# Attention: unnormalized probabilities into the product with v, made token by token, divided as it leaves its bank, and transposed

## The reference, cut to what matters

```python
s_lat = jnp.where(mask[None, :, None, None], s_lat, -jnp.inf)
s_ctx = jnp.einsum('bnqkgd,bskd->bnkgqs', qb, k_ctx).astype(jnp.float32) * ATTN_SCALE
logits = jnp.concatenate([s_lat, s_ctx, sink_logits(sink, s_lat.shape)], axis=-1)
p = jax.nn.softmax(logits, axis=-1).astype(v.dtype)
o = (jnp.einsum('bnkgqs,bnskd->bnqkgd', p[..., :n_band], vb)
     + jnp.einsum('bnkgqs,bskd->bnqkgd', p[..., n_band:-1], v_ctx))
return o.reshape(B, L, ATTN_DIM) @ w_o
```

## Time and profile before

| what | value |
|---|---|
| median of 3 runs | 3303.78 us (3301.16 to 3306.16) |
| profiled execution, its own time | 3303.78 us |
| span of the profiled execution | 3301.9 us |
| PE busy | 3066.8 us, 93% |
| PE weight loads | 2819.7 us, 85% |
| DVE busy | 2154.3 us, 65% |
| ACT busy | 1140.0 us, 35% |

### The profile page before, as it was taken

One profiled execution on the slowest core, in us unless ns is written; L12 is line 12 of the kernel. 1 busy time (PEld: TensorE's weight loads), 2 busy tenths in 40 slices (PEclk: granted clock), 3 DMA queues, 4 the chain that ended last, 5 costly groups with the idle time before them and its releaser, 6 DMA issues. The chain is left out here.

```text
span 3301.9 us, 48081 instructions
## 1 busy us (share of the span) xinstructions
PE 3066.8 (93%) x19222; PEld 2819.7 (85%) x19222; DVE 2154.3 (65%) x2879; ACT 1140.0 (35%) x1941; POOL 574.5 (17%) x578
## 2 busy tenths in 40 slices
PE   5999869999999999999999998679999999969999
PEld 4999658999899898998999897468998999858998
DVE  4776486777776656776876535657777777485444
ACT  3222454223422424223322433234224222454222
POOL 1112101112111111112111102642112112201001
PEclk8999899999999999999999998679999999999999
DMA  7666414666565445665665443024665666313443
GB/s 262 201 206 183 142 46 133 195 218 188 182 196 171 110 127 186 197 208 169 199 209 148 122 126 103 15 68 155 218 195 153 218 208 199 107 43 90 128 128 96
DMA packets 565507, 515.75 MB, mean 156 GB/s; under 512 B 42965, under 2 KB 499238, under 8 KB 563494
## 3 DMA queue, kind: packets, MB, share of 16 engines
q1 hardware_dynamic: 565286, 512.68, 50.8%
HBM read 509.37 MB, written 3.24 MB: 155 GB/s over the span
## 5 line engine op out<-in xcount | busy, mean ns | idle before, releaser
L1342 PE MATMUL bank<-h_hi,w_hi 128*128 128x384 f32 x3328 | 1114.9, 335 | 0.0
L1344 PE MATMUL bank<-h_hi,w_lo 128*128 128x384 f32 x3328 | 1113.7, 335 | 0.0
L1343 PE MATMUL bank<-h_lo,w_hi 128*128 128x384 f32 x3328 | 1113.2, 334 | 0.0
L1745 DVE TENSOR_TENSOR w_lo<-raw,w_hi 128x1024 fp32r<-128x1024 f32 x648 | 805.4, 1269 | 418.2 <-ACT w_hi L1591 413.0
L1591 ACT ACTIVATE w_hi<-raw 128x1024 fp32r<-128x1024 f32 x648 | 679.4, 1060 | 995.7 <-PE bank L1375 483.4
L1767 DVE SCALAR_TENSOR_TENSOR fold<-ada_raw,cond,fold 128x1024 f32<-128x1024 f32 x462 | 638.6, 1439 | 0.0
L1342 PEld LDWEIGHTS bank<-h_hi,w_hi 128*128 128x128 f32 x3328 | 625.1, 188 | 6.9 <-issue 1.2
L1343 PEld LDWEIGHTS bank<-h_lo,w_hi 128*128 128x128 f32 x3328 | 625.0, 188 | 5.8
L1344 PEld LDWEIGHTS bank<-h_hi,w_lo 128*128 128x128 f32 x3328 | 624.9, 188 | 0.0
L2057 POOL TENSOR_TENSOR h_lo<-tmp,h_hi 128x384 fp32r<-128x384 f32 x176 | 283.9, 1613 | 1799.6 <-DVE h_hi L1793 1799.6
L1371 PE MATMUL bank<-w_hi,h_hi 128*128 128x512 f32 x1056 | 334.2, 397 | 0.0
(11 more groups left out here) (198 smaller groups left out, 2422.4 us busy)
## 6 DMA issues: line engine op xcount, KB each, us to landing
raw<-w_ffn_in SPq DMA_DIRECT2D x352, 512.0 KB, 5.0
ada_raw<-w_ada SPq DMA_DIRECT2D x272, 512.0 KB, 4.2
raw<-w_ffn_out SPq DMA_DIRECT2D x176, 512.0 KB, 4.5
raw<-w_hgrn_in SPq DMA_DIRECT2D x40, 512.0 KB, 4.9
g_rows<-g_dram SPq DMA_DIRECT2D x12, 1024.0 KB, 6.8
raw<-w_attn_qkv SPq DMA_DIRECT2D x24, 512.0 KB, 5.9
raw<-w_conv_in SPq DMA_DIRECT2D x24, 512.0 KB, 4.7
ada_first<-w_ada SPq DMA_DIRECT2D x16, 512.0 KB, 10.8
```

The costliest lines, as they stand in the source:

```text
L1342: mm(out, wh, h_hi[:, k, :], start=(k == 0), stop=False)
L1343: mm(out, wh, h_lo[:, k, :], start=False, stop=False)
L1344: last = mm(out, wl, h_hi[:, k, :], start=False, stop=(k == DC - 1))
L1745: V.tensor_tensor(w_lo[:, b % RING, :], raw[:, b % RAW, :], w_hi[:, b % RING, :].bitcast(F32), ALU.subtract).then_inc(w_lo_made, 1)
```

## The change

The exponentials go to PE undivided. `turn_probs` waits for `prob_made` and no more for `p_normed`. `values(c)` has its operands exchanged: the transposed probabilities, 128x128, are the weights, 64 columns of v move, and the result has tokens on partitions and both heads' 2 x 64 features beside each other, for three token blocks, always in bank 6. The 14 products remain 14; `tile_position` is gone. DVE's `normalize` is replaced by `inverse(c)`, the sums and the reciprocal of both heads into `over`, and `scale_out(c)`, one multiplication of 384 elements from bank 6 into `tmp` with the reciprocals broadcast. PE's new `turn_out(c)` transposes the three 128x128 blocks of `tmp` into bank 7, from which ACT and DVE make `o_hi` and `o_lo`. The loops have one step more (`DC + 3`).

```diff
@@ pe_core
-            pe.wait_ge(p_normed, n + 1)
+            pe.wait_ge(prob_made, n + 1)
...
-            if c >= 2:
-
-                pe.wait_ge(o_lo_made, DC * mi + c - 1 + CREDIT)
-            bank = psum[6 + c % 2]
+            if c >= 1:
+
+                pe.wait_ge(o_scaled, DC * a + c)
             cols = slice(g * HD, (g + 1) * HD)
-            key = [vt[:, 1, cols], vt[:, 2, cols], vc[:, cols]]
+            latent = [vt[:, 1, cols], vt[:, 2, cols], vc[:, cols]]
             for x in range(2):
...
+                for b, (kt, keys) in enumerate(((0, latent), (3, [vt[:, 0, cols]]), (4, latent))):
+                    lo = P * b + HD * x
+                    for k, key in enumerate(keys):
+                        last = mm(psum[6][:, lo:lo + HD], pt[(2 * c + x) % 3][:, (kt + k) * P:(kt + k + 1) * P], key,
+                                  start=(k == 0), stop=(k == len(keys) - 1))
             last.then_inc(pv_done, 1)
 
-        for j in range(DC + 2):
+        def turn_out(c):
+            pe.wait_ge(o_scaled, DC * a + c + 1)
+            if c >= 1:
+
+                pe.wait_ge(o_lo_made, DC * mi + c + CREDIT)
+            for b in range(3):
+                last = nc.tensor.transpose(psum[7][:, TILE_OF[b] * P:(TILE_OF[b] + 1) * P],
+                                           tmp[:, c % 2, b * P:(b + 1) * P], ident)
+            last.then_inc(o_turned, 1)
+
+        for j in range(DC + 3):
             if j < DC:
                 scores(j)
+            if j >= 3:
+                turn_out(j - 3)
             if 1 <= j <= DC:
                 turn_probs(2 * j - 2)
-            if j >= 2:
+            if 2 <= j < DC + 2:
                 values(j - 2)
@@ act_core
-        for j in range(DC + 2):
+        for j in range(DC + 3):
+            if j >= 3:
+                c = j - 3
+                act.wait_ge(o_turned, DC * a + c + 1)
+                A(o_hi[:, c, :], psum[7][:, 0:T], ACT.Copy).then_inc(mix_hi_made, 1)
...
-            if j >= 2:
-                c = j - 2
-                act.wait_ge(pv_done, DC * a + c + 1)
-                A(o_hi[:, c, :], psum[6 + c % 2][:, 0:T], ACT.Copy).then_inc(mix_hi_made, 1)
@@ dve_core
-        def normalize(h):
...
+        def inverse(c):
+            dve.wait_ge(prob_made, HEADS * a + 2 * c + 2)
...
+            r = over[:, c % 2, :, 0:3]
+            V.tensor_tensor(r, soft[:, :, 6:9], soft[:, :, 9:12], ALU.add).then_inc(soft_step, 1)
+            dve.wait_ge(soft_step, 2 * (DC * a + c) + 1)
+            V.reciprocal(r, r).then_inc(soft_step, 1)
+
+        def scale_out(c):
+            dve.wait_ge(pv_done, DC * a + c + 1)
+            dve.wait_ge(soft_step, 2 * (DC * a + c) + 2)
+            if c >= 2:
+                dve.wait_ge(o_turned, DC * a + c - 1)
+            r = over[:, c % 2, :, 0:3].rearrange("p x b -> p b x").unsqueeze(3).to_broadcast([P, 3, 2, HD])
+            V.tensor_tensor(tmp[:, c % 2, :].rearrange("p (b x d) -> p b x d", b=3, x=2),
+                            psum[6][:, 0:T].rearrange("p (b x d) -> p b x d", b=3, x=2), r,
+                            ALU.mult).then_inc(o_scaled, 1)
...
             if j < DC:
                 maxima(2 * j + 1)
-                normalize(2 * j)
+            if 2 <= j < DC + 2:
+                scale_out(j - 2)
             if 1 <= j <= DC:
                 copy_probs(2 * j - 1)
+            if j >= 3:
+                c = j - 3
...
+                V.tensor_tensor(o_lo[:, c, :], psum[7][:, 0:T], o_hi[:, c, :].bitcast(F32),
+                                ALU.subtract).then_inc(o_lo_made, 1)
             if j < DC:
-                normalize(2 * j + 1)
...
+                inverse(j)
```

More of the change, by code:

```diff
@@ L355, in build @@
     SEG_AT = (0, T, T + P)
+    TILE_OF = (1, 0, 2)
     KEYS = sum(SEG)
@@ L378, in build @@
     soft = put("soft", [P, 2, 16])
+    over = put("over", [P, 2, 2, 4])
     rot_m = attn_k[:, 0:P]
@@ L390, in build @@
     sink8_made, score_done, score_read, neg_made = sem("sink8_made"), sem("score_done"), sem("score_read"), sem("neg_made")
-    prob_made, soft_step, p_normed, pt_done = sem("prob_made"), sem("soft_step"), sem("p_normed"), sem("pt_done")
-    pt_copied_v, pt_copied_a, pv_done = sem("pt_copied_v"), sem("pt_copied_a"), sem("pv_done")
+    prob_made, soft_step, o_scaled, pt_done = sem("prob_made"), sem("soft_step"), sem("o_scaled"), sem("pt_done")
+    pt_copied_v, pt_copied_a, pv_done, o_turned = sem("pt_copied_v"), sem("pt_copied_a"), sem("pv_done"), sem("o_turned")
     STEPS = HEADS + 3
@@ L536, in values @@
             pe.wait_ge(pt_copied_a, HEADS * a + 2 * c + 2)
-            if c >= 2:
-                pe.wait_ge(o_lo_made, DC * mi + c - 1 + CREDIT)
-            bank = psum[6 + c % 2]
+            if c >= 1:
+                pe.wait_ge(o_scaled, DC * a + c)
             cols = slice(g * HD, (g + 1) * HD)
-            key = [vt[:, 1, cols], vt[:, 2, cols], vc[:, cols]]
+            latent = [vt[:, 1, cols], vt[:, 2, cols], vc[:, cols]]
             for x in range(2):
[L544 to L554, removed]
-            last.then_inc(pv_done, 1)
-        for j in range(DC + 2):
+                for b, (kt, keys) in enumerate(((0, latent), (3, [vt[:, 0, cols]]), (4, latent))):
[3 more added lines that the diff above has]
+                                  start=(k == 0), stop=(k == len(keys) - 1))
+            last.then_inc(pv_done, 1)
+        def turn_out(c):
[7 more added lines that the diff above has]
+        for j in range(DC + 3):
             if j < DC:
                 scores(j)
+            if j >= 3:
+                turn_out(j - 3)
             if 1 <= j <= DC:
                 turn_probs(2 * j - 2)
-            if j >= 2:
+            if 2 <= j < DC + 2:
                 values(j - 2)
@@ L766, in copy_probs @@
             V.tensor_copy(pt[h % 3][:, 0:512], psum[4][:, :]).then_inc(pt_copied_v, 1)
-        def normalize(h):
[L769 to L780, removed]
+        def inverse(c):
+            dve.wait_ge(prob_made, HEADS * a + 2 * c + 2)
+            if c >= 2:
+                dve.wait_ge(o_scaled, DC * a + c - 1)
+            r = over[:, c % 2, :, 0:3]
[5 more added lines that the diff above has]
+            dve.wait_ge(soft_step, 2 * (DC * a + c) + 2)
+            if c >= 2:
+                dve.wait_ge(o_turned, DC * a + c - 1)
[3 more added lines that the diff above has]
+                            ALU.mult).then_inc(o_scaled, 1)
+        for j in range(DC + 3):
             if j < DC:
@@ L786, in dve_core @@
                 maxima(2 * j + 1)
-                normalize(2 * j)
+            if 2 <= j < DC + 2:
+                scale_out(j - 2)
             if 1 <= j <= DC:
                 copy_probs(2 * j - 1)
-            if j < DC:
-                normalize(2 * j + 1)
[L792 to L796, removed]
+            if j >= 3:
+                c = j - 3
+                dve.wait_ge(mix_hi_made, DC * mi + c + 1)
+                V.tensor_tensor(o_lo[:, c, :], psum[7][:, 0:T], o_hi[:, c, :].bitcast(F32),
+                                ALU.subtract).then_inc(o_lo_made, 1)
+            if j < DC:
+                inverse(j)
         dve.wait_ge(out_stored, 16 * stores_until(s + 1))
```

## The result

The changed kernel took 3322.15 us (median of 4 runs, 3321.32 to 3325.38) against 3303.05 us before (4 runs, 3301.16 to 3306.16): a ratio of 1.0058, 95% interval 1.0043 to 1.0073. It is slower by 0.6%, 19 us. The forecast was 3308 with a range to 3316, so it missed, on the side of its first rival and beyond that rival's price. Steps and queues came out nearly as laid out; TensorE's clock at the cores' end did not.

The account below looks back on a forecast made before the run. The prediction took DVE to bound the attention cores before and PE's loop over ACT after. Start, steps and end summed to +2.6 us in the first core and +1.5 in the second: 3303.8 + 4.1 = 3308, range 3302 to 3316.

Parts of the forecast that it names:

- What bounds the kernel now: Attention cores: DVE, busy 7.17 of 7.47 us, sets the step; all working is on 133.7 us of both cores.
- DVE, part by part: DVE's work in a step falls to 5.67 us; if DVE alone decided, 1.8 us a step saved.
- PE, part by part: PE's step becomes 6.92 us, values taking 3.12 instead of 1.53, so PE becomes the bound.
- rival 2: Gaps between PE blocks belong to semaphore waits: 0.15 kept per new block, loop 7.5, time 3313; chance 0.13.
- Rival 3: In values, 128-column loads hide and 64 moving columns decide: 1.5 us, step 6.1, time 3289; chance 0.04.
- The loop that closes: Round of turn_probs, values, turn_probs, exponentials and copy makes a step 7.22 us; five steps 36.1 instead of 37.3.
- the 0.03 among its signs: Expected in the profile after: in each step, PE's turn_probs waits for ACT's pt by 0.03.
- The start: Steps 0 to 2 of each core: 0.94 us shorter, 14.0 in the first core, 14.4 in the second.
- rival 4: Low-clock stretch in the start moves: 0.8 us a core gained or 3.6 lost; inside the range, no own chance.
- The end: Last step's first maxima to projection: 18.56 us instead of 13.84 and 15.0, clock taken as staying at 1.00.
- Rival 1: Clock falls in the new end too: values(6) 3.1 us more per core, 4 with longer drop, 3315; chance 0.14.
- The sum: Cores 68.7 and 69.1 us against 66.1 and 67.6: +4.1 us on 3303.8, so 3308.

Follow-up runs that it names:

- e3_no_divide: Kernel before with the multiplications of pr by the reciprocals left out, turn_probs waiting for the exponentials alone, old values: 3293.4 us, ratio 0.9967.
- e2_wide_v: Changed kernel with each product of values streaming v's 64 columns twice, 128 moving columns: 3312.3 us, ratio 1.0025 against the kernel before.
- e5_both_orders: Changed kernel with ACT's copy of head 2j-1 before head 2j+1's exponentials and DVE's o_lo before its copy: 3297.8 us, ratio 0.9981 against the kernel before.
- e4_act_order: Changed kernel with only ACT's copy of head 2j-1 moved ahead of the exponentials of head 2j+1: 3302.2 us, one run, no ratio.
- e9_late_turns: e5_both_orders with turn_out(6) behind values(7) and turn_out(7) behind the projection's first block on PE: 3295.9 us, ratio 0.9976 against the kernel before.
- e1_fill_end: Changed kernel with unread identity transposes (11, 5, 11, 10) in PE's four pauses at the core's end: 3310.0 us, ratio 1.0017 against the kernel before.
- e11_wide_end: Changed kernel with v streamed twice, 128 moving columns, in values(6) and values(7) alone: 3312.4 us, ratio 1.0021 against the kernel before.
- e8_before_fill: Kernel before with 22 identity transposes in PE's one long pause at the core's end, before turn_probs(14): 3302.8 us, ratio 0.9994.

## Why the prediction was wrong, point by point

- **What bounds the kernel now**: right. DVE is busy 7.17 of the 7.47 us, and e3_no_divide shows that relieving it helps: 6.94.
- **DVE, part by part**: right. scale_out 0.56 against 0.55; DVE busy 5.71 of a step against 5.67.
- **PE, part by part**: right. 28 records in 3.08 us, 0.110 each, against 3.12 (28 x 0.112 is 3.14), and e2_wide_v shows that the load decides. The gap belongs to the shape change and not to the wait: none stands before `values`; rival 2 falls. Rival 3 wanted 1.5 us for the 28 records and falls too. Scores with its gap measured 1.73 against 1.80. PE's own step is 6.82 (e5_both_orders) against 6.92.
- **The loop that closes**: right, 7.22 forecast and 7.29 measured. PE's wait for ACT is 0.29 us, which is the forecast's 7.22 - 6.92 = 0.30; the 0.03 among its signs does not fit its own sum. Five steps took 37.0 in the first core, where one step was 7.5 and one 7.6, and 36.5 in the second, against 36.1. e4_act_order removes the loop by one line.
- **The start**: 14.0 and 14.4 forecast, 13.7 and 13.0 measured. One low stretch of the second core's start did not come, rival 4's case. Its price was 0.8; between the two cores of the changed kernel, one with it and one without, it is 0.7 in the start and 1.2 up to the last step's maxima, and 1.6 in e9_late_turns.
- **The end**: here it failed, in the sentence "so I take the clock as staying at 1.00". The work and waits were right: with the clock up the end is 18.67 us (e1_fill_end) against 18.56, and the first two pauses were 1.34 and 0.64 against 1.5 and 0.8. The clock fell in both cores.
- **Rival 1** named the mechanism with a chance of 0.14 and a price of 3 to 4 us a core. The price was 7 us a core (13.9 over both), and another 1.2 in the projection's first group. It was sized for values(6) alone, as the low stretches of before, 3.4 and 6.8 us, would cover it; their `values` moved 128 columns. The new low stretch, 20.5 us, also covers turn_probs(15), turn_out(6), values(7) and turn_out(7). This is the mis-sized term, and e11_wide_end shows what it hangs on: with 128 moving columns it is 3.4 us. The forecast held against a fall that turn_out(5) splits the pause, and it did; but the 1.42 us of PE work in the 3.40 us ahead of the fall, where the kernel before had 0.49, did not prevent the fall.
- **The sum** without the clock: 3308, against 3310.0 for e1_fill_end, whose cores take 137.5 us together against 137.8. Part of that agreement is luck: its starts are 1.3 us shorter than forecast and its steps 0.8 longer. The gap of 12.2 us in time to the changed kernel is less than the 13.9 and 2.4 at the ends: in e1_fill_end's trace what lies outside is 6 us longer, 4.3 of them between the cores, a stretch that varies from run to run (e8_before_fill, above).

On the column tiles, the Trainium skill (TensorEngine Tiling, "When to Use Tiling") advises, where the right side has 64 columns or fewer, to swap the operands and tile the columns. The kernel before does that; the change undoes it. The traces agree with the page: 28 records in 1.53 us before, 3.08 after.

## What to carry to other kernels

Here a record with a 128-column fp32 stationary side cost its load, 0.110 us, with 64 moving columns, and 0.112 with 128. So a swap of operands that leaves a narrow moving side and gives up column tiles has to be priced by loads. Ends of a pipeline, where PE works and waits in turns, are to be priced at both levels of the clock: the ends of the changed kernel took 18.7 us at the one and 25.7 with the low stretch. And where relieving one engine gains less than its row says, the round of waits over a third engine's queue order may be what is left: moving one copy ahead of an exponential took 0.47 us off a step here (e4_act_order), the edit under study 0.18.

## What the hardware showed that I had not expected

- A fallen clock stayed at 0.50 for 20.5 us, although PE was busy without a hole for the first 6.8 of them, mostly with products that moved 64 columns; the same loads with 128 moving columns had it back after 3.4 us (e11_wide_end, both cores). The Trainium skill (TensorE: Matmul & The Clock Gate, "Loop structure matters more than you think") has back-to-back matmuls stay warm and waits make PE cold. The falls after pauses agree with it. The 6.8 us of products without a wait that stayed at 0.50 do not, and there the measurement decides.
- Streaming 128 instead of 64 columns behind an fp32 load of 128 was nearly free, 0.04 to 0.05 us for 28 records, and so a cheap way to get a fallen clock back; it did not prevent every fall (3.4 us low in e2_wide_v's second core).
- Transposes that nobody reads, put in waits of 0.6 to 1.3 us, made the changed kernel 12 us faster (3322.2 to 3310.0).
